# Branch products as three float32r products, and the mixers of a decoder trunk in another order

## The chip, the cores and the metric

The kernel runs on one core of a Trainium2 chip. A core has TensorE (PE, matmuls; PEld is its weight load), VectorE (DVE), ScalarE (ACT), GpSimd (POOL) and SyncE (SP), each with an instruction queue of its own that it works off in order, and 16 DMA engines. The metric is the device time of one execution in microseconds (us).

## What is computed

One layer of a decoder trunk for 512 prompt tokens and 8 x 8 sample tokens (576 together) of width 1024. Four token mixers A to D read one projection, each is projected by a 512 x 1024 matrix, and a sigmoid gate per branch and channel weights the result. Cross attention and a mixture of experts follow; the change does not touch them.

```python
z = jnp.einsum('btd,de->bte', x, p['w_in']) + p['b_in']
u, v, yg, xb, c, q, f, i, go, gz = jnp.split(z, SPLIT_POINTS, axis=-1)
o_a, v_rows = chunk_sgu(u, v, ...)            # A: u * (causal 128x128 mix of LN(v))
xc, conv_new = causal_conv(xb, ...)
h, h_new = rg_lru(xc, h0, ...)                # B: convolution, sigmoids, scan
o_b = jax.nn.gelu(yg) * h
o_c, pool_new = pool_mixer(c, ...)            # C: windows 2, 4, 8, 16
o_d, s_new = hgrn2(q, f, i, go, s0, lb, ...)  # D: gated recurrence, 4 heads
branches = jnp.stack([o_a, o_b, o_c, o_d], axis=2)
proj = jnp.einsum('btgc,gcd->btgd', branches, p['w_branch'])
gates = jax.nn.sigmoid(gz.reshape(B, T, N_BRANCH, D_MODEL))
y = jnp.einsum('btd,de->bte', jnp.sum(gates * proj, axis=2), p['w_out'])
```

## The kernel before

Tokens lie along the free dimension, 576 columns in two halves of 288, channels on the 128 partitions. The mixer phase is a list of steps, `mixer_steps()`, that every engine walks through in the same order; each engine does its own part of a step and waits on semaphores for the others.

- `z` steps project one chunk of 128 channels for one half: 24 matmuls of 128x288 (8 k-tiles, three float32r products each: hi x hi, hi x lo, lo x hi), `split_products`. The weight chunk (1024 x 128, 512 KB) is loaded by SyncE into one of four buffers once the chunk four back is used, and split into a rounded part (`z_weights_hi`) and a rest (`z_weights_lo`) by GpSimd. ScalarE writes the result out with its function (Gelu for `yg`, Silu for `q` and `go`). `kv` steps are float32 products with the memory's weights.
- `hgrn` steps are the four heads of mixer D (called heads 1 to 4 here, numbered 0 to 3 in the code): `prep`, `keys`, `state`, `diag`, `lev0` to `lev8`, `out`, `norm`. At `keys` TensorE transposes an operand that ScalarE and VectorE make; at `lev n` it makes the product of level n-1, from what VectorE wrote at the same step after ScalarE's exponential of the step before. The `z` and `kv` steps fill TensorE between them: `rest` is dealt out over the heads in proportion to the steps' weights.
- Then come `pool` (C), `lru` (B) and `sgu` (A) steps with `merge` units between them, and a loop with the remaining units.
- A `merge` unit (i, u) is half of one chunk of 128 output channels for one branch: a gate product (24 float32r matmuls, bank 0 or 1), a branch product (4 float32 matmuls of 128x288, two records each, bank 2 or 3), ScalarE's sigmoid into `gate`, and VectorE's product, added to `mer`. Branches go D, C, B, A (3 - i). There are 64 units; 32 are written out (`PEEL = 2`), 32 are in the loop. Branch weights have four buffers and are used as they land.
- GpSimd's queue holds the weight splits and, for the pool mixer, the copies into the padded rows `cpad`, which wait for `hg_done`, the output of the four heads.

The diff changes `psum_schedule`, `z_units`, `mixer_steps`, `z_plan` and each engine's `merge_unit`.

## Time and profile before

| | us |
|---|---|
| median of 3 runs | 1592.98 |
| lowest, highest | 1591.44, 1595.31 |
| profiled execution | 1593.02 |
| its span | 1591.2 |
| TensorE busy | 1436.9 (90%) |
| VectorE busy | 782.9 (49%) |
| ScalarE busy | 514.3 (32%) |
| GpSimd busy | 298.1 (19%) |
| weighted products of the branches (512 records) | 134.5 |

The span is the time from the first to the last instruction of the profiled execution; the 1.8 us between it and that execution's own time lie around it. Matmul ends are modelled and matmuls are pipelined, so the distance between two starts tells more than the length of one record. A wait is idle time of an engine, with the instruction that released it.

### The profile page before, as it was taken

The page shows a single profiled execution, that of the slowest core. Times are in us where ns is not written, and L with a number is a line of the kernel's source. Part 1 is how long each engine was busy: PE and PEld are TensorE (multiplying, and loading weights), DVE is VectorE, ACT ScalarE, POOL GpSimd, SP SyncE. Part 2 cuts the span into 40 slices and gives each one's busy share as a digit, 9 for nine tenths or more (in the row PEclk, how much of TensorE's full clock was granted, in tenths as well). Part 3 has the DMA queues.
Part 4 walks back from the last instruction along what each step waited for, and adds up shares of the span by engine and source line. Part 5 has one row for each costly group of instructions (what it writes and reads, how often), then busy time and mean ns, then how long its engine had stood idle before and what let it go on. Part 6 is the DMA issues. An engine that isn't in the chain of part 4 may idle for free.

```text
span 1591.2 us, 20322 instructions
## 1 busy us (share of the span) xinstructions
PE 1436.9 (90%) x8037; PEld 1199.5 (75%) x8037; DVE 782.9 (49%) x1162; ACT 514.3 (32%) x772; POOL 298.1 (19%) x234
## 2 busy tenths in 40 slices
PE   5998889899789788999999989999897799999985
PEld 4887888888778676989998867765685677777762
DVE  6204437362545467632221430244336688887786
ACT  1123341513431343311110011333123566666640
POOL 5111132313314131323332000001000100000030
PEclk9999999998899898999999989999998899999997
DMA  9302232422122121242225311235254699999941
GB/s 328 99 27 74 79 96 77 118 84 78 53 82 71 49 80 40 62 130 80 80 59 195 124 54 53 80 116 207 62 222 153 240 381 394 390 390 396 391 152 61
DMA packets 182172, 234.89 MB, mean 148 GB/s; under 512 B 6224, under 2 KB 125705, under 8 KB 181953
## 3 DMA queue, kind: packets, MB, share of 16 engines
q1 hardware_dynamic: 154848, 170.90, 31.7%
q0 software_dynamic: 12384, 43.56, 8.0%
q10 hardware_dynamic: 14849, 19.16, 3.5%
q8 instruction: 63, 1.03, 0.3%
q14 instruction: 28, 0.23, 0.0%
HBM read 213.98 MB, written 19.36 MB: 147 GB/s over the span
## 4 chain that ended last, share of the span: by engine, by line
PE 48%; DVE 3%; DMA 2%; ACT 2%; issue 1%; POOL 0%; POOLq 0%; DVEq 0%; SPq 0%; ACTq 0%
PE bank L1114 46%; ACT kv_t L744 1%; PE bank L1606 1%; DMA ring<-in_w_out_dram 1%; DMA early_rows<-expert_rows,ints 0%; DVE x_tok L2490 0%; DVE small L1739 0%; DVE x_tok L2496 0%; POOL early_rows L2673 0%; DMA xg<-x_scratch,table 0%; PE bank L1598 0%; PE bank L1138 0%; PE bank L1422 0%; DVE x_tok L2398 0%; DVE x_tok L1751 0%
## 5 line engine op out<-in xcount | busy, mean ns | idle before, releaser
L1114 PE MATMUL bank<-x_hi,z_weights_hi 128*128 128x288 f32 x960 | 307.1, 320 | 9.1 <-DVE ob L1903 5.5
L1114 PE MATMUL bank<-x_lo,z_weights_hi 128*128 128x288 f32 x960 | 290.5, 303 | 0.0
L1114 PE MATMUL bank<-x_hi,z_weights_lo 128*128 128x288 f32 x960 | 290.1, 302 | 0.0
L2232 DVE TENSOR_TENSOR expert_weights_lo<-mring,expert_weights_hi 128x2048 fp32r<-128x2048 f32 x80 | 181.8, 2287 | 54.2 <-ACT expert_weights_hi L1007 54.0
L1114 PEld LDWEIGHTS bank<-x_hi,z_weights_hi 128*128 128x128 f32 x960 | 189.0, 197 | 15.6 <-issue 6.3
L1114 PEld LDWEIGHTS bank<-x_lo,z_weights_hi 128*128 128x128 f32 x960 | 188.6, 196 | 2.6
L1114 PEld LDWEIGHTS bank<-x_hi,z_weights_lo 128*128 128x128 f32 x960 | 187.7, 195 | 0.0
L1007 ACT ACTIVATE expert_weights_hi<-mring 128x2048 fp32r<-128x2048 f32 x80 | 153.4, 1918 | 78.7 <-PE bank L1114 78.7
L2544 POOL CAST z_weights_hi<-z_weights 128x1024 fp32r<-128x1024 f32 x60 | 65.7, 1094 | 592.3 <-PE bank L1114 365.8
L2546 POOL TENSOR_TENSOR z_weights_lo<-z_weights,z_weights_hi 128x1024 fp32r<-128x1024 f32 x60 | 147.4, 2456 | 6.4 <-POOL z_weights_hi L2544 2.9
L1114 PE MATMUL bank<-ob,branch_weights 128*128 128x288 f32 (+1 forms) x512 | 134.5, 405 | 0.0
L906 ACT ACTIVATE gate<-bank,pc 128x288 f32<-128x288 f32 x64 | 31.8, 501 | 255.8 <-PE bank L1114 255.7
L1114 PE MATMUL bank<-expert_weights_hi,xgT_hi 128*128 128x512 f32 x256 | 106.1, 414 | 3.1 <-DVE xgT_lo L2375 3.1
L1114 PEld LDWEIGHTS bank<-ob,branch_weights 128*128 128x128 f32 x512 | 93.3, 189 | 20.3
L1114 PE MATMUL bank<-expert_weights_lo,xgT_hi 128*128 128x512 f32 x256 | 100.5, 393 | 0.0
L1114 PE MATMUL bank<-expert_weights_hi,xgT_lo 128*128 128x512 f32 x256 | 100.3, 392 | 0.0
L2065 DVE TENSOR_TENSOR prod<-gate,bank 128x288 f32<-128x288 f32 x48 | 21.8, 454 | 154.9 <-PE bank L1114 142.5
L1114 PE MATMUL bank<-ring,oT 128*128 128x256 f32 (+1 forms) x320 | 71.2, 381 | 1.1 <-DVE o_rows L2122 1.1
L2656 POOL DMA_INDIRECT xg<-x_scratch,table x16 | 24.8, 1552 | 230.7 <-PE bank L1606 221.0
L1114 PEld LDWEIGHTS bank<-ring,oT 128*128 128x128 f32 (+1 forms) x320 | 56.7, 179 | 13.3 <-issue 2.2
L1114 PE MATMUL bank<-yT,ring 128*128 128x288 f32 x256 | 64.4, 416 | 0.8 <-ACT yT L744 0.8
L1114 PEld LDWEIGHTS bank<-yT,ring 128*128 128x128 f32 x256 | 49.9, 195 | 15.0 <-ACT yT L744 0.9
(419 smaller groups left out, 2303.7 us busy)
## 6 DMA issues: line engine op xcount, KB each, us to landing
mring<-in_e_wg_dram SPq DMA_DIRECT2D x32, 1024.0 KB, 8.5
mring<-in_e_wu_dram SPq DMA_DIRECT2D x32, 1024.0 KB, 9.4
mring<-in_e_wd_dram SPq DMA_DIRECT2D x32, 1024.0 KB, 8.0
z_weights<-in_w_in_dram SPq DMA_DIRECT2D x60, 512.0 KB, 3.9
branch_weights<-in_w_branch_dram SPq DMA_DIRECT2D x32, 256.0 KB, 3.2
kv_k<-in_cache_mem_k_dram POOLq DMA_DIRECT2D x8, 1024.0 KB, 7.6
kv_v<-in_cache_mem_v_dram POOLq DMA_DIRECT2D x8, 1024.0 KB, 5.5
expert_rows<-y_out ACTq DMA_DIRECT2D x14, 512.0 KB, 6.9
```

Of the source, the lines that this page charges most:

```text
L744: act.activation(dst, ps[0:rows, cols[0]:cols[1]] if len(dst.shape) == 2 else ps[0:rows, cols[0]:cols[1]].rearrange("p (a b) -> p a b", a= ...
L906: act.activation(gate[:, b, :], bank[b][:, 0:HALF], ACT.Sigmoid, bias=pc[:, bass.ds(col, 1)]).then_inc(free[b], 1)
L1007: act.activation(m_hi[n % NHI][:], mring[:, chunk_slot[split[n]], :], ACT.Copy).then_inc(m_hi_done, 1)
L1114: return pe.matmul(out, lhsT, rhs, start=start, stop=stop)
L1606: m = pe.transpose(bank[2 + s][:, P * e:P * e + P], xg[:, u, P * c:P * c + P], ident)
L2065: dve.tensor_tensor(prod[:, half, :], gate[:, half, :], bank[nb][:, 0:HALF], ALU.mult).then_inc(free[nb], 1)
L2232: dve.tensor_tensor(m_lo[slot][:], mring[:, slot, :], m_hi[n % NHI][:].bitcast(F32), ALU.subtract).then_inc(m_lo_done, 1)
L2544: pool.tensor_copy(w_hi[hi][:], w_raw[raw][:]).then_inc(g_hi_done, 1)
L2546: pool.tensor_tensor(w_lo[raw][:], w_raw[raw][:], w_hi[hi][:].bitcast(F32), ALU.subtract).then_inc(g_lo_done, 1)
L2656: return pool.indirect_dma_start(xg[:, u, :], None, x2_d, bass.IndirectOffsetOnAxis(ap=index, axis=0))
```

## The change

It does five things.

1. The branch product of a unit becomes 12 float32r matmuls: branch output and branch weights are both split into a rounded part and a rest. ScalarE writes the rounded branch (`branch_hi`, new steps `split`), VectorE the rest (`ob_lo`), per chunk k of four; GpSimd splits each chunk of branch weights behind the gate weights. The branch weights have two buffers instead of four.
2. The spatial mixer (A) moves from last to first: its norms behind `norm` of head 1, its products and outputs into head 3, its splits before and behind `prep` of head 4. Twelve merge units of branch A (chunks 0, 1, 2, 4, 5, 6) stand between the steps of head 4, the other four behind it.
3. The branches are merged in the order A, D, C, B; C is split after each pool output, B after each scan.
4. The loop is gone, all 64 units are written out. The product is written over `gate` and then added to `mer`; only units of the first branch write `mer` at once.
5. `u` is projected before `yg`; the conv, pool and LRU states are written between units.

```diff
+BRANCHES = (0, 3, 2, 1)
+EARLY_D = (0, 1, 2, 4, 5, 6)
+MERGE_D = (EARLY_D + (3, 7),) + (tuple(range(8)),) * 3
...
+    for j in range(KW):
+        rest += [("sgu", "product", j), ("sgu", "out", j)]
+    rest += [("split", 0, j) for j in range(KW)]
+    rest += [("merge", 0, u) for u in range(2 * len(EARLY_D))]
...
+    at = own.index(("hgrn", "norm", 0)) + 1
+    own[at:at] = [("sgu", "norm", j) for j in range(NT + 1)]
...
+    steps += [("split", 1, h) for h in range(KW)]
+    merge(16 - 2 * len(EARLY_D))
...
-        steps.append(("pool", "out", j))
+        steps += [("pool", "out", j), ("split", 2, j)]
...
-        if j:
-            steps.append(("sgu", "norm", 2 * j - 1))
...
+            def branch_hi(i, k):
+                if i == 0:
+                    act.wait_ge(sgu_done, KW)
+                    act.wait_ge(out_stored, 16)
+                elif i == 1:
+                    act.wait_ge(hg_done, KW)
...
+                act.activation(ob_hi[i % 2][:, k, :], ob[:, BRANCHES[i], k, :], ACT.Copy).then_inc(ob_hi_done, 1)
...
+            def branch_lo(i, k):
+                dve.wait_ge(ob_hi_done, splits.index((i, k)) + 1)
+                dve.tensor_tensor(ob_lo[:, BRANCHES[i], k, :], ob[:, BRANCHES[i], k, :], ob_hi[i % 2][:, k, :].bitcast(F32),
+                                  ALU.subtract).then_inc(ob_lo_done, 1)
...
-                    m = mm(bank[2 + half][:, 0:HALF], p_raw[d % 4][:, k, :], rhs, k == 0, k == KW - 1)
+                pe.wait_ge(ob_lo_done, splits.index((i, KW - 1)) + 1)
+                pe.wait_ge(p_lo_done, m + 1)
+                    pairs = ((p_hi[m % 2], hi), (p_hi[m % 2], lo), (p_lo[m % 2], hi))
...
+            def split_gate_weights(m):
+                used(chunk_last(m - 2, "mg") if m >= 2 else z_last[z_split[z_split_last(m)]])
+                split_weights(m % 2, at % ZRING, len(z_split) + m + 1)
+                pool.wait_ge(p_landed[m % 2], 16 * (m // 2 + 1))
+                pool.tensor_copy(p_hi[m % 2][:], p_raw[m % 2][:]).then_inc(p_hi_done, 1)
+                pool.tensor_tensor(p_lo[m % 2][:], p_raw[m % 2][:], p_hi[m % 2][:].bitcast(F32), ALU.subtract).then_inc(p_lo_done, 1)
...
+                elif step[0] == "merge" and step[2] % 2:
+                    split_gate_weights(8 * step[1] + step[2] // 2 + 2)
```

VectorE's queue from the output of head 3 to the keys' operand of head 4 (the row that writes `ob` with `tmp` is the head's output, the last row the keys' operand), before:

```order
L1901 SCALAR_TENSOR_TENSOR tmp<-tmp,pc 128x576
L1903 TENSOR_TENSOR ob<-ob,tmp 128x576
L1797 SCALAR_TENSOR_TENSOR tmp<-f_all,tmp 128x576
L1798 SCALAR_TENSOR_TENSOR tmp<-cst,tmp 128x576
L1801 TENSOR_TENSOR tmp<-tmp 128x512
L1803 TENSOR_TENSOR tmp<-tmp 128x64
L1809 TENSOR_TENSOR f_all<-q_all,tmp 128x576
L1810 COPY small<-tmp 128x4
L1811 COPY small<-tmp 128x8
L1813 TENSOR_TENSOR tmp<-tmp 128x576
```

The same place now, from the head's output on; `conv_odd` rows are the last spatial output.

```order
L1910 TENSOR_TENSOR ob<-ob,tmp 128x576
L2046 TENSOR_TENSOR conv_odd<-bank,sgu_rows 128x512
L2050 TENSOR_TENSOR conv_odd<-bank,sgu_rows 128x64
L2057 TENSOR_TENSOR ob<-ob,conv_odd 128x576
L2079 TENSOR_TENSOR branches_lo<-ob,branch_hi_72 128x576
L1804 SCALAR_TENSOR_TENSOR tmp<-f_all,tmp 128x576
L1805 SCALAR_TENSOR_TENSOR tmp<-cst,tmp 128x576
L2079 TENSOR_TENSOR branches_lo<-ob,branch_hi_72 128x576 x3
L2067 TENSOR_TENSOR mer<-gate,bank 128x288
L1808 TENSOR_TENSOR tmp<-tmp 128x512
L1810 TENSOR_TENSOR tmp<-tmp 128x64
```

A spatial output, four splits and a merge have come between the head's output and the keys; the keys' operand stands four rows further on.

VectorE's queue between two level steps of head 4 (`tmp<-tmp` and `tmp<-q_all,tmp` are the cuts of a level, `mer` is the merge of a unit), before:

```order
L1863 TENSOR_TENSOR tmp<-tmp 128x4x64
L1864 TENSOR_TENSOR tmp<-tmp 128x4x64
L1863 TENSOR_TENSOR tmp<-tmp 128x8x32
L1864 TENSOR_TENSOR tmp<-tmp 128x8x32
L1877 TENSOR_TENSOR tmp<-q_all,tmp 128x4x64
L1878 TENSOR_TENSOR tmp<-tmp 128x4x64
```

And now:

```order
L2067 TENSOR_TENSOR mer<-gate,bank 128x288
L1870 TENSOR_TENSOR tmp<-tmp 128x8x32
L1871 TENSOR_TENSOR tmp<-tmp 128x8x32
L1884 TENSOR_TENSOR tmp<-q_all,tmp 128x4x64
L1885 TENSOR_TENSOR tmp<-tmp 128x4x64
```

The merge of the unit that fills TensorE at `lev0` stands ahead of the cuts of the next level.

GpSimd's queue up to the first two padded rows of the pool mixer, before:

```order
L2544 CAST z_weights_hi_62<-z_weights_54 128x1024
L2546 TENSOR_TENSOR z_weights_lo_58<-z_weights_54,z_weights_hi_62 128x1024
L2562 MEMSET cpad 128x15
L2570 COPY cpad<-ob 128x512
L2571 COPY cpad<-pst 128x8x15
L2572 COPY cpad<-ob 128x8x8
```

And now:

```order
L2601 CAST branch_weights_hi_69<-branch_weights_65 128x512
L2603 TENSOR_TENSOR branch_weights_lo_67<-branch_weights_65,branch_weights_hi_69 128x512
L2555 CAST z_weights_hi_63<-z_weights_55 128x1024
L2557 TENSOR_TENSOR z_weights_lo_59<-z_weights_55,z_weights_hi_63 128x1024
L2601 CAST branch_weights_hi_70<-branch_weights_66 128x512
L2603 TENSOR_TENSOR branch_weights_lo_68<-branch_weights_66,branch_weights_hi_70 128x512
L2578 MEMSET cpad 128x15
L2586 COPY cpad<-ob 128x512
L2587 COPY cpad<-pst 128x8x15
L2588 COPY cpad<-ob 128x8x8
```

Before, the padded rows stand behind the split of one chunk of gate weights, now behind the splits of gate and branch weights of the ninth and the tenth chunk.

## Rows read from the trace of the kernel before

**Rows 1.** Windows: stretch, length, busy (x) of PE, PEld, DVE, ACT, POOL, clock, DMA.
```profile
132.00:404.00 272.00, 244.96 (x1799) 233.92 (x1799) 125.85 (x202) 94.83 (x142) 72.57 (x40) 0.95 0.30 87
404.00:473.50 69.50, 54.03 (x367) 50.28 (x365) 35.80 (x68) 27.63 (x40) 14.13 (x8) 0.92 0.25 70
473.50:538.20 64.70, 55.32 (x305) 48.28 (x305) 31.29 (x74) 10.05 (x15) 24.12 (x27) 0.92 0.22 61
538.20:692.00 153.80, 141.47 (x808) 122.41 (x808) 100.37 (x164) 53.74 (x76) 42.70 (x24) 0.94 0.22 62
692.00:861.30 169.30, 167.90 (x1035) 153.65 (x1036) 40.03 (x68) 18.49 (x36) 51.81 (x33) 0.98 0.30 92
168.30:171.70 3.40, 3.40 (x17) 3.40 (x16) 3.37 (x2) 0.35 (x1) 3.32 (x2) 0.50 0.31 93
```

**Rows 2.** TensorE's waits, 130 to 960 us: total, times, longest.
```profile
PE bank L1114 <- DVE tmp L1878: 20.9, 11, 3.3
PE bank L1232 <- DVE tmp L1813: 18.5, 4, 5.5
PE bank L1114 <- DVE tmp L1981: 12.0, 2, 6.5
PE bank L1114 <- DVE ob L1903: 5.5, 1, 5.5
PE bank L1114 <- DVE conv_odd L1981: 4.0, 1, 4.0
...
PE bank L1114 <- issue: 2.8, 2, 1.9
...
PE bank L1371 <- DVE tmp L2038: 2.2, 2, 1.6
...
PE bank L1114 <- ACT gate L906: 1.4, 1, 1.4
```

**Rows 3.** Timeline of TensorE in the closing loop: start, us, instruction.
```profile
762.45 2.10 PE L1114 MATMUL bank<-ob,branch_weights 128*128 x8
764.17 0.51 PE L1114 MATMUL bank<-x_hi,z_weights_hi 128*128 128x288 f32 x1
764.52 0.29 PE L1114 MATMUL bank<-x_lo,z_weights_hi 128*128 128x288 f32 x1
```

**Rows 4.** Timeline of GpSimd: one weight chunk split in two.
```profile
476.81 1.12 POOL L2544 CAST z_weights_hi<-z_weights 128x1024 fp32r<-128x1024 f32 x1
478.01 2.39 POOL L2546 TENSOR_TENSOR z_weights_lo<-z_weights,z_weights_hi 128x1024 fp32r<-128x1024 f32 x1
```

**Rows 5.** Part 6 of the page: DMA issues, KB each, us to landing.
```profile
branch_weights<-in_w_branch_dram SPq DMA_DIRECT2D x32, 256.0 KB, 3.2
```

**Rows 6.** Timeline of VectorE: one output of the spatial mixer, first and last row.
```profile
683.78 0.68 DVE L2038 TENSOR_TENSOR tmp<-bank,sgu_rows 128x512 f32<-128x512 f32 x1
...
684.69 0.76 DVE L2049 TENSOR_TENSOR ob<-ob,tmp 128x576 f32<-128x576 f32 x1
```

**Rows 7.** Tile x_hi, ScalarE: count, shortest, median, longest in ns.
```profile
L811 ACT ACTIVATE x_hi<-xT x8: 667/668/684, 49.6 to 53.6; 128x576 fp32r<-128x576 f32 x8
```

**Rows 8.** Timeline of ScalarE in prep of head 4.
```profile
399.76 1.28 ACT L837 ACT_TABLE_LOAD   x1
401.06 0.78 ACT L837 ACTIVATE tmp<-tmp,small 128x576 f32<-128x576 f32 x1
```

**Rows 9.** Timeline of VectorE at a level of head 4.
```profile
436.43 0.42 DVE L1878 TENSOR_TENSOR tmp<-tmp 128x256 f32<-128x256 f32 x1
436.76 0.68 DVE L1887 TENSOR_TENSOR att_m<-bank,cst 128x512 f32<-128x512 f32 x1
```

**Rows 10.** Timeline of VectorE: first and last row of the fourth pool window.
```profile
513.21 0.90 DVE L1923 TENSOR_TENSOR csum<-cpad 128x710 f32<-128x710 f32 x1
...
518.28 0.22 DVE L1941 COPY att<-cpad 128x120 f32<-128x120 f32 x1
```

**Rows 11.** Timeline of VectorE: start of the third LRU convolution.
```profile
593.27 2.57 DVE L1977 TENSOR_SCALAR tmp<-xpad,pc 128x512 f32<-128x512 f32 x1
```

More of the change, by code:

```diff
@@ L133, in psum_schedule @@
             (low if step[0] in ("z", "kv") else high)(name)
-    for b in range(4):
-        count[b] += (4 - PEEL) * 8
     turn["low"] = 0
@@ L214, in mixer_steps @@
             steps.append(rest.pop(0))
-    units = [("merge", i, u) for i in range(PEEL) for u in range(16)]
+    at = [steps.index(step) for step in (("hgrn", "state", KW - 2), ("sgu", "out", 0), ("sgu", "out", KW - 1),
+                                         ("hgrn", "keys", KW - 1))]
+    assert at == sorted(at) and steps.index(("merge", 0, 0)) > steps.index(("hgrn", "norm", KW - 2))
+    units = [("merge", 0, u) for u in range(2 * len(EARLY_D), 16)] + [("merge", i, u) for i in range(1, 4) for u in range(16)]
+    late = []
     def merge(count):
         for _ in range(count):
-            if units:
-                steps.append(units.pop(0))
+            steps.append(units.pop(0))
+            if steps[-1] == ("merge", 1, 15):
+                steps.extend(late)
+                late.clear()
+    steps += [("split", 1, h) for h in range(KW)]
+    merge(16 - 2 * len(EARLY_D))
     for j in range(KW):
@@ L242, in mixer_steps @@
         steps.append(("lru", "scan", j))
-        if j < KW - 1:
-            steps.append(("sgu", "norm", 2 * j))
+        (late if units[0][1] == 1 else steps).append(("split", 3, j))
         if j < KW - 1:
@@ L247, in mixer_steps @@
         merge(1)
-    merge(1)
-    for j in range(KW):
-        steps.append(("sgu", "product", j))
-        merge(1)
-        steps.append(("sgu", "out", j))
+    steps.append(("states",))
     merge(len(units))
-    steps.append(("states",))
     return steps
@@ L290, in step_units @@
         return ["oc", "op", "oq"]
-    if step[1] != "product":
+    if step[0] in ("merge", "split") or step[1] != "product":
         return []
@@ L303, in z_plan, with branch_splits @@
                     names.append(name)
-                last[name] = step_units(step)[0]
+                last[name] = f"mg{step[1]}_{step[2]}" if step[0] == "merge" else step_units(step)[0]
     return names, last
+def branch_splits():
+    return [step[1:] for step in mixer_steps() if step[0] == "split"]
 def weight_plan():
```

244 lines of the change are left out of this document (113 added, 131 removed).

## Prediction

> **What bounds the kernel now.** First the stretches of the span, then TensorE's waits by cause, then single timelines. TensorE is busy for nearly all of each mixer stretch [rows 1]: the four heads of the gated recurrence run from 132 to 473.5 us, pool, LRU and spatial mixers with 32 units from 473.5 to 692, the closing loop with the other 32 to 861.3. So time is TensorE work, plus its waits, plus what the halved clock costs. From 130 to 960 us it waits 20.9 us in 11 places for the level products' operands (tmp L1878), 18.5 in 4 for the keys (L1813), 12.0 and 4.0 for the LRU convolution, 5.5 for the last head's output, 2.8 before pool products (issue), 2.2 and 0.6 for the last spatial rows, 1.4 for a gate [rows 2]. The granted clock, read as its missing share times each stretch, costs 0.05 x 272 + 0.08 x 69.5 + 0.08 x 64.7 + 0.06 x 153.8 + 0.02 x 169.3 = 37 us [rows 1]. Outside 132 to 861 nothing changes.
>
> **The products.** A unit is a gate product of 24 float32r matmuls and a branch product of 4 float32 ones, 8 records. In the loop the 8 start at 762.45 and the next unit at 764.17: 1.72 us. The first float32r start after them takes 0.35 us to the next, where such starts are else 0.13 apart [rows 3]: 0.22 more. Twelve float32r matmuls at 0.1325 are 1.59, so a unit falls by 1.72 + 0.22 - 1.59 = 0.35, and 64 of them by 22.4. Twelve units now stand alone between small float32 products and pay such a change of type again: about 2 back. Term: **-20.5** (bounds -16, if the pace is 0.14, and -24).
> The trace shows 8 records in 1.72 us for 4 products, 0.43 each, 3.25 float32r steps. The Trainium skill, FP8 and Floating Point Precision, TensorE Precision Notes, says that true FP32 makes four passes. By that a product were 4 x 0.1325 = 0.53 us, the 64 units would save 256 x 0.1325 = 34, and the sum would be some 13 lower. The trace does not agree.
> GpSimd also splits the branch weights. Its cast of 128x1024 takes 1.12 and its subtraction 2.39 [rows 4], so half the size is 0.56 + 1.2; a chunk costs 3.5 + 1.8 + about 0.3 = 5.6 us against two units, 2 x 4.8 = 9.6. The branch weights have two buffers and load when the product two chunks back is done, 3.2 us to landing [rows 5]: split some 6 us after that product, wanted 12.8 after it. Hidden, about 7 to spare.
>
> **The keys, and the start of head 4.** The keys' operand comes only after ScalarE has emptied the fill ahead of it, so heads 2 and 3 keep waits of 4.3 and 5.5. Ahead of head 4 it is another thing. Fills are dealt by count, and count now includes steps without matmul work; after `norm` of head 3 TensorE has only a spatial product (1.35) and the first gate product (3.2). The branch product needs all four splits of the spatial branch, which stand around `prep` on ScalarE and VectorE. From the end of the norm product: head output 5.0 (5.5 in [rows 2], less 0.4 of a table load that can now run ahead); last spatial output on VectorE 1.67 (683.78 to 685.45), to 6.6 [rows 6]; ScalarE copy of 128x576 0.67 [rows 7]; `prep` on ScalarE with three table loads of 1.28, and four activations of 0.6 to 0.8 [rows 8], to 13.9; VectorE's two operations 2.1; three subtractions 0.76 each, to 18.4. TensorE is free at 4.6: it waits 13.9. The product, at half clock, ends at 21.4, and behind it VectorE's gate product, keys and ScalarE's exponential reach 25.0: 3.6 more. Keys: 4.3 + 5.5 + 13.9 + 3.6 + the unchanged 4.3 = 31.6, against 18.5: **+13.1** (bounds +6 and +18).
> The row has table loads at 1.28 us. The Trainium skill, ScalarE: Activation LUTs, What ACT_TABLE_LOAD costs, gives about 2.7; by it the chain's three loads would put 4 us more here. The measured row decides.
>
> **The levels.** Head 1 and 2 get denser fills and wait where a slot is empty: 3.7 (such a wait with a table load in it was 3.3 from the modelled end [rows 2]) + 1.7 and 1.8 + 1.2 = 8.4. In head 3 the fill is used up at the third level; from there VectorE's chain sets the pace, one level being four cuts of 0.42 and a mask and sum of 0.68 each, 3.1 us [rows 9], 3.8 at the small levels, against 0.8 to 1.35 of TensorE work, with three spatial outputs of 1.67 in VectorE's queue. Step by step: 0.1 + 3.0 + 1.1 + 4.0 + 1.3 + 3.5, and 0.9 + 0.6 at output and norm = 14.5. In head 4 every fill is now a unit whose product VectorE must merge before it comes to the next level: after the branch product 0.45 until it starts, 0.45 merge, four cuts 1.4 = 2.4 us in which TensorE has nothing. Five such, 0.9 and 1.5 where no fill stands, 0.7 at the state: 15.1. Sum 38.0 against 20.9: **+17.1** (bounds +8, if VectorE ran ahead at half of them, and +24).
> At the end of head 4 four units cover the 5.5: **-5.5**.
>
> **Pool.** GpSimd now writes the padded rows behind the split of the tenth chunk, whose branch weights load only after the eighth chunk's last product: 3.5 to land, 1.8 + 0.3 split, 1.2 pads, 2.5 window = 9.5 from there, TensorE filled for 4.8: wait 5.2 with the drain. For the next three VectorE's queue between a unit and the next pool product is merge 0.95 (two operations, one before), output 1.0, then new: ScalarE's copy 0.67 with hand-overs 0.2, subtraction 0.76, then the window, 3.5, 4.4, 5.3 (the last is 513.21 to 518.50 [rows 10], the others one and two sums of 0.9 shorter, as is the first above with 2.5). Less the filling unit of 4.8 that gives 3.6, 4.1, 4.7. Together 17.6 against 2.8: **+14.8** (bounds +6 and +19).
>
> **LRU and states.** The spatial norms no longer stand ahead of the second and third convolution, 3.5 us each, and no gate waits for them; the subtraction that replaces them is 0.76, and a fill is 0.3 shorter. First product 7.2, then 0.8, 1.2, 1.2 = 10.4 against 12.0 + 4.0 + 1.4: **-7.0**. The states go between units: 0.5 for 2.8, **-2.3**.
>
> **Sum:** -20.5 + 13.1 + 17.1 - 5.5 + 14.8 - 7.0 - 2.3 - 7 + 5 + 2 = +9.7. The profiled execution's 1593.0 becomes 1602.7, said as 1603; its 1593.02 (span 1591.2) is within 0.1 of the median of the three, 1592.98, so nothing is scaled.
>
> **The rivals.**
> *The waits close.* A fill in head 4 is longer now (4.8 for 3.2) and may hide the level chain. For it: VectorE is only half busy there, 35.8 of 69.5 us, and TensorE idles 15 [rows 1], which the new fills could take. It decides if VectorE reaches a level's cuts before the fill ends; the order of its queue, merge first, speaks against. Then +17.1 falls to about 0 and half of the keys' term and its clock go: 1603 - 17 - 7 - 3 = 1576; with half of that, 1589. **Faster**, 0.17.
> *Four passes.* If each float32 product were worth four float32r steps, the term of the products would be 34 and the time 1603 - 13.4 = 1589.6, on the edge of faster and same; rows 3 show 3.25 steps, 3.7 with the change of type. That is the rule of FP8 and Floating Point Precision in the Trainium skill. 0.04, half to each side.
> *It evens out.* One of the two terms, pool or levels, lies at its lower bound (9 less each) and the other between: 1603 - 9 = 1594, down to 1590. Same, 0.15.
> *GpSimd sets the pace.* If loading and splitting took over 9.6 us a chunk, 32 chunks would each be late. From rows 4 and 5 it is 5.6 and 3.2 in parallel with spare; at 10.5 it would be 32 x 0.9 = 29 more, 1631. 0.04.
> *The forecast,* waits outweigh products, 0.60.
>
> **How the numbers follow.** Slower by over 0.2% (3.2 us, about what a measurement of this kernel can tell) is 0.60 + 0.04 = 0.64; same 0.15 + 0.02 = 0.17; faster 0.17 + 0.02 = 0.19. The range leaves out the fully closed waits and the GpSimd case, and takes waits closed by somewhat over half (-18) and the upper bounds of levels, pool and clock together (+7 + 4 + 9, of which I take 17): 1585 to 1620.
>
> **What would show it.** Right: branch products of 12 records 0.13 apart; a TensorE wait of over 10 us in the first branch product; waits near 2.4 us after each unit in head 4; 4 to 5 us before each pool product; the two LRU waits of 5.5 and 4.0 nearly gone; a closing run of 20 units at 4.8. Wrong: head 4 without waits above 2, pool products without wait, a closing pace above 5.

## The result and the profile after

The changed kernel takes 1634.6 us (median of four runs, 1632.1 to 1640.0) against 1594.1 for the kernel before beside it: ratio 1.0258, interval 1.0227 to 1.029. The profiled execution took 1634.13, its span 1632.3. Forecast were 1603 and a range of 1585 to 1620: slower was right, the size was not. Between the two profiled executions the loss is 41 us and not 10.

The stretches of the changed kernel, in the windows' columns of [rows 1]. Its mixer phase ends some 41 us later, so the same clock times hold earlier work; the granted clock is what to read first.

```profile
136.00:404.00 268.00, 247.93 (x1853) 239.30 (x1852) 107.70 (x184) 86.90 (x134) 80.94 (x46) 0.96 0.32 90
404.00:473.50 69.50, 40.47 (x253) 36.83 (x251) 40.16 (x70) 29.95 (x39) 11.98 (x8) 0.77 0.15 41
473.50:538.20 64.70, 51.80 (x299) 47.70 (x300) 27.33 (x48) 20.29 (x25) 16.07 (x12) 0.79 0.16 46
538.20:692.00 153.80, 117.17 (x731) 107.68 (x730) 68.22 (x126) 32.48 (x49) 57.39 (x50) 0.84 0.16 47
692.00:861.30 169.30, 158.02 (x1131) 151.78 (x1131) 102.22 (x142) 53.83 (x80) 84.04 (x60) 0.97 0.30 87
```

Until 404 little differs. From 404 to 692 TensorE is busy 209 of 288 us and granted 0.77 to 0.84, where [rows 1] have 251 of 288 and 0.92 to 0.94: the loss is waits there, and with them clock. (Half clock, below, is a granted clock of 0.50, 1.2 GHz for 2.4.) GpSimd is busy 157 us from 473.5 to 861 for 119.

TensorE's waits from 100 to 1000 us, in total, times, longest, to be laid beside [rows 2] (the line numbers are those of the changed kernel: L1885 are the level operands, L1820 the keys, L1988 the convolutions, "issue" is here the waits before the four pool products, 21.2 together, and one of 0.5 elsewhere):

```profile
PE bank L1129 <- DVE tmp L1885: 36.9, 16, 7.3
PE bank L1129 <- issue: 21.6, 5, 6.1
PE bank L1247 <- DVE tmp L1820: 17.4, 4, 5.7
PE bank L1129 <- DVE branches_lo L2079: 13.3, 1, 13.3
PE bank L1129 <- DVE tmp L1988: 11.6, 2, 7.8
PE bank L1129 <- DVE conv_odd L1988: 6.8, 2, 4.1
```

The levels grew by 16, the pool products from 2.8 to 21.2, the first branch product waits 13.3, and the convolutions, forecast at 10.4 in all, wait 18.4.

Three starts of a gate product in the closing run, one unit each:

```profile
830.71 0.30 PE L1129 MATMUL bank<-x_hi,z_weights_hi 128*128 128x288 f32 x1
835.49 0.29 PE L1129 MATMUL bank<-x_hi,z_weights_hi 128*128 128x288 f32 x1
840.23 0.30 PE L1129 MATMUL bank<-x_hi,z_weights_hi 128*128 128x288 f32 x1
```

They are 4.78 and 4.74 apart. Before, the same distance is this:

```profile
799.98 0.51 PE L1114 MATMUL bank<-x_hi,z_weights_hi 128*128 128x288 f32 x1
805.08 0.51 PE L1114 MATMUL bank<-x_hi,z_weights_hi 128*128 128x288 f32 x1
```

5.10. A unit gained 0.34, as forecast (0.35), and the first matmul no longer takes 0.51: the change of type is gone.

Head 4's start and the pool products on TensorE (the wait and its releaser in brackets):

```profile
473.45 0.61 PE L1129 MATMUL bank<-branch_hi,branch_weights_hi 128*128 128x288 f32 x1 [13.31 <-DVE branches_lo L2079]
473.86 0.44 PE L1129 MATMUL bank<-branches_lo,branch_weights_hi 128*128 128x288 f32 x1
...
479.72 0.69 PE L1247 MATMUL bank<-cst,tmp 128*128 128x128 f32 x2 [3.02 <-DVE tmp L1820]
```

```profile
611.39 2.37 PE L1129 MATMUL bank<-ob,wp 128*128 128x512 f32 x4 [4.33 <-issue]
...
647.85 2.37 PE L1129 MATMUL bank<-ob,wp 128*128 128x512 f32 x4 [5.84 <-issue]
667.52 2.36 PE L1129 MATMUL bank<-ob,wp 128*128 128x512 f32 x4 [6.12 <-issue]
```

The branch product that ends the 13.3 us wait runs at half clock (0.24 between starts), and so does each of the four pool products after its wait (the second, left out here, waits 4.86): 2.4 us, where the same product took 1.26 before.

### The profile page after: what moved, and what is told of

Read it like the earlier page. It is cut to its first block, busy times and chain, and to the rows that moved or that the text cites. A ratio compares the mean times of both kernels' runs of the same rounds, so it can differ in the third digit from the quotient of the medians.

```text
span 1632.3 us, 20440 instructions
## 1 busy us (share of the span) xinstructions
PE 1431.0 (88%) x8293; PEld 1216.2 (75%) x8293; DVE 807.8 (49%) x1178; ACT 538.1 (33%) x799; POOL 364.4 (22%) x298
## 4 chain that ended last, share of the span: by engine, by line
PE 53%; DVE 8%; issue 4%; ACT 4%; DMA 2%; POOL 0%; POOLq 0%; DVEq 0%; SPq 0%; ACTq 0%
PE bank L1129 50%; ACT kv_t L742 1%; PE bank L1613 1%; DMA ring<-in_w_out_dram 1%; DVE mer L2074 1%; DMA early_rows<-expert_rows,ints 0%; DVE tmp L2002 0%; DVE x_tok L2500 0%; DVE small L1746 0%; DVE x_tok L2506 0%; ACT L906 0%; DMA xg<-x_scratch,table 0%; DVE gate L2072 0%; POOL early_rows L2689 0%; PE bank L1605 0%
## 5 line engine op out<-in xcount | busy, mean ns | idle before, releaser
L1129 PE MATMUL bank<-x_hi,z_weights_hi 128*128 128x288 f32 x960 | 298.6, 311 | 1.9 <-POOL z_weights_lo L2557 1.3
L906 ACT ACTIVATE gate<-bank,pc 128x288 f32<-128x288 f32 x64 | 31.5, 500 | 239.9 <-PE bank L1129 229.8
L1129 PE MATMUL bank<-branch_hi,branch_weights_hi 128*128 128x288 f32 x256 | 76.1, 297 | 13.4 <-DVE branches_lo L2079 13.3
L2072 DVE TENSOR_TENSOR gate<-gate,bank 128x288 f32<-128x288 f32 x48 | 21.7, 452 | 124.5 <-PE bank L1129 88.9
L1129 PE MATMUL bank<-tmp 128*128 128x128 f32 (+1 forms) x248 | 41.9, 320 | 39.4 <-DVE tmp L1885 36.9
L1129 PE MATMUL bank<-branches_lo,branch_weights_hi 128*128 128x288 f32 x256 | 76.1, 297 | 0.0
L1129 PE MATMUL bank<-branch_hi,branch_weights_lo 128*128 128x288 f32 x256 | 75.9, 296 | 0.0
L1129 PEld LDWEIGHTS bank<-tmp 128*128 128x128 f32 (+1 forms) x248 | 36.0, 221 | 44.8 <-DVE tmp L1885 40.2
```

Of the source, the lines that this page charges most:

```text
L906: act.activation(gate[:, b, :], ps[:, 0:HALF], ACT.Sigmoid, bias=pc[:, col:col + 1]).then_inc(fr, 1)
L1129: return pe.matmul(out, lhsT, rhs, start=start, stop=stop)
L2072: dve.tensor_tensor(gate[:, half, :], gate[:, half, :], ps[:, 0:HALF], ALU.mult).then_inc(fr, 1)
```

## Experiments

### The order, the products and the splits taken apart

Three kernels stand between the kernel before and the changed one. The first has the new order with the old products.

```diff
-                pe.wait_ge(ob_lo_done, splits.index((i, KW - 1)) + 1)
-                pe.wait_ge(p_lo_done, m + 1)
+                pe.wait_ge(p_landed[m % 2], 16 * (m // 2 + 1))
...
-                    pairs = ((p_hi[m % 2], hi), (p_hi[m % 2], lo), (p_lo[m % 2], hi))
+                    ins = mm(ps[:, 0:HALF], p_raw[m % 2][:, k, :], ob[:, BRANCHES[i], k, cols], k == 0, k == KW - 1)
...
-                act.activation(ob_hi[i % 2][:, k, :], ob[:, BRANCHES[i], k, :], ACT.Copy).then_inc(ob_hi_done, 1)
...
-                pool.tensor_copy(p_hi[m % 2][:], p_raw[m % 2][:]).then_inc(p_hi_done, 1)
```

> The changed kernel's order with the branch products of before: four float32 matmuls from the branch output and the landed weights, no split of branch or branch weights on ScalarE, VectorE or GpSimd. Theory (the products save about 20 us, the splits cost nearly as much in waits): products +20.5; the wait of 13.3 in the first branch product falls to about 2, but the keys of head 4 then wait some 7 longer, -5; pool waits 1.65 shorter each, -6; LRU waits back near 0 to 1, -7; clock -3: about 1634, the same as the changed kernel. Rival (the splits are hidden and the order alone makes the waits): all of the 20 us come on top, 1650 to 1655. Other rival (the products gained less than 20, for the clock was halved beside many of them): below 1620.

Measured 1607.0 (ratio to before 1.0087, 1.0064 to 1.0111). The theory (1634) and the first rival (1650) were wrong. The time lies in the band of the second rival, below 1620, and the next run bears out that the products gain less than 20, but not through the clock, as it had it. The changed kernel is 27.7 slower than its own order with the old products: the splits cost more than the products give back. What is left to the order alone is 13.5.

The second adds TensorE's side of the change alone (the edit against the run before it).

```diff
-                    ins = mm(ps[:, 0:HALF], p_raw[m % 2][:, k, :], ob[:, BRANCHES[i], k, cols], k == 0, k == KW - 1)
+                    for n in range(3):
+                        ins = mm(ps[:, 0:HALF], x_hi[:, k, 0:P], (x_hi, x_lo)[n % 2][:, k, cols], k == 0 and n == 0,
+                                 k == KW - 1 and n == 2)
```

> The run with float32 products, with twelve float32r matmuls of 128x288 in the place of each four float32 ones, but from operands that are there anyway (the input's rounded part and rest), so no split of branch or weights is made and the branch products are left out of the result. It has TensorE's gain from the change without its price. Theory (0.35 us a unit, forecast -20.5 with bounds -16 and -24): 1607 - 20 = 1587, unit distance in the closing run 4.75 for 5.1. Rival (shorter fills only make the waits longer: in head 4 and between pool and LRU steps 40 units fill the waits, and only the closing units give their gain in full): 1607 - 10 = 1597.

Measured 1593.9 (ratio 0.9995, 0.9978 to 1.0011): 13.1 below the run before it, between theory and rival. In the closing run a unit takes 4.77 for 5.11, so TensorE's work fell by some 20, but in the stretches where another engine sets the pace a shorter unit only uncovers more of the wait. Half clock is not the reason: from 100 to 1000 us it holds for 102 us in the run before and 99 in this one. The waits of the two, first with float32 products, then with the stand-in:

```profile
PE bank L1121 <- DVE tmp L1880: 32.4, 16, 4.0
PE bank L1239 <- DVE tmp L1815: 21.9, 4, 7.5
PE bank L1121 <- DVE tmp L1983: 9.1, 2, 6.7
PE bank L1121 <- issue: 8.0, 5, 3.2
...
PE bank L1121 <- DVE conv_odd L1983: 1.6, 2, 1.0
```

```profile
PE bank L1121 <- DVE tmp L1882: 33.3, 15, 4.0
PE bank L1239 <- DVE tmp L1817: 22.4, 4, 7.9
PE bank L1121 <- issue: 10.8, 5, 3.9
PE bank L1121 <- DVE tmp L1985: 9.9, 2, 7.1
PE bank L1121 <- DVE conv_odd L1985: 3.1, 2, 1.7
```

The lines are 0.5 to 2.8 longer, together 6.5, which is about what the 20 lack.

The third has the splits of the branches (ScalarE, VectorE) as in the changed kernel, but not GpSimd's splits of the branch weights.

```diff
-                    pairs = ((p_hi[m % 2], hi), (p_hi[m % 2], lo), (p_lo[m % 2], hi))
+                    pairs = ((x_hi, hi), (x_hi, lo), (x_hi, hi))
...
-                pool.tensor_copy(p_hi[m % 2][:], p_raw[m % 2][:]).then_inc(p_hi_done, 1)
...
-                pool.tensor_tensor(p_lo[m % 2][:], p_raw[m % 2][:], p_hi[m % 2][:].bitcast(F32), ALU.subtract).then_inc(p_lo_done, 1)
```

> The changed kernel without GpSimd's cast and subtraction of the branch weights; the branch products take the input's rounded part as weights, so their result is not the branch products. TensorE's work and the splits of the branches on ScalarE and VectorE are as in the changed kernel. It stands between the stand-in run (1593.9, no split at all) and the changed kernel (1634.6). Theory (GpSimd's share is stretched VectorE rows, which cost 11.6 us for the subtraction alone, the branch splits' share is the hole before the first branch product and the queue before the pool products): GpSimd 15 to 18 of the 40.7, so 1617 to 1620; the fifth level wait of head 3 (7.3) back at 4.0, the last three LRU waits under 3 each. Rival (the subtraction was all of it and the cast costs nothing): 1623. Other rival (GpSimd is nearly all): below 1610.

Measured 1608.2 (ratio 1.0109, 1.0076 to 1.0141). So the 40.7 between the stand-in and the changed kernel divide into 14.3 for the branch splits and 26.4 for GpSimd. (The run's interval leaves some 5 us of play in this division.) The theory had 15 to 18 for GpSimd and the first rival 1623; the time lies in the band of the second rival, below 1610. GpSimd's two operations, 1.9 us a chunk and never themselves waited for in the closing run, are the dearer part. The longest level wait is back at 4.0, and the convolutions wait 13.9 for 18.4:

```profile
PE bank L1127 <- DVE tmp L1883: 33.4, 15, 4.0
...
PE bank L1127 <- issue: 15.5, 5, 5.5
PE bank L1127 <- DVE tmp L1986: 10.5, 2, 7.7
PE bank L1127 <- DVE branches_lo L2077: 10.2, 1, 10.2
PE bank L1127 <- DVE conv_odd L1986: 3.4, 2, 2.0
```

(The wait for `branches_lo` is 13.3 in the changed kernel and 10.2 here, but the gate product ahead of it ran at full clock there and at half clock here. VectorE is ready at the same point after the head's output in both; half clock inside a stretch that waits anyway cost nothing here.)

### GpSimd beside VectorE

VectorE and then GpSimd in the changed kernel, where the second and the third convolution are made late (start, us, instruction):

```profile
706.22 0.46 DVE L2072 TENSOR_TENSOR gate<-gate,bank 128x288 f32<-128x288 f32 x1
706.71 1.96 DVE L2074 TENSOR_TENSOR mer<-mer,gate 128x288 f32<-128x288 f32 x1
...
710.30 1.29 DVE L1988 SCALAR_TENSOR_TENSOR conv_odd<-xpad,pc,conv_odd 128x64 f32<-128x64 f32 x1
...
739.98 2.36 DVE L1988 SCALAR_TENSOR_TENSOR tmp<-xpad,pc,tmp 128x64 f32<-128x64 f32 x1
```

```profile
705.85 2.50 POOL L2557 TENSOR_TENSOR z_weights_lo<-z_weights,z_weights_hi 128x1024 fp32r<-128x1024 f32 x1
...
709.91 1.60 POOL L2603 TENSOR_TENSOR branch_weights_lo<-branch_weights,branch_weights_hi 128x512 fp32r<-128x512 f32 x1
...
739.59 2.67 POOL L2557 TENSOR_TENSOR z_weights_lo<-z_weights,z_weights_hi 128x1024 fp32r<-128x1024 f32 x1
```

The add into `mer`, 0.46 elsewhere, starts at 706.71 and ends at 708.67; GpSimd's subtraction ends at 708.35. The 128x64 row, 0.28 elsewhere, starts at 710.30 and ends at 711.59; GpSimd's ends at 711.51. At 739.98 it is 2.36, to 742.34; GpSimd ends at 742.26. A VectorE operation with two operands in SBUF that starts inside one of these GpSimd operations ends just behind it, while the product from a bank at 706.22 is not touched. That holds for the whole stretch from 130 to 1000 us: of 68 such rows that start inside a cast or a subtraction of weights with over 0.3 us of it left, 67 are at least 0.15 us longer than the shortest of their form and end 0.1 to 1.1 us behind GpSimd; of 46 rows that read a bank in the same place none is longer. The longest level wait, 7.33, ends behind such rows too: a cut of 0.46 starts at 430.60 and takes 2.48, inside a subtraction that ends at 432.76. The Trainium skill, SBUF — State Buffer, section SBUF: two separate sides, calls the pair of ports that VectorE and GpSimd share an exclusive lock for the whole instruction, for VectorE operations with two SBUF inputs among others. These rows agree, to 0.3, 0.1 and 0.1 us.

Shortening one of GpSimd's operations (1.3 us to 0.25) tests it with all other work in place:

```diff
-                pool.tensor_tensor(p_lo[m % 2][:], p_raw[m % 2][:], p_hi[m % 2][:].bitcast(F32), ALU.subtract).then_inc(p_lo_done, 1)
+                pool.tensor_tensor(p_lo[m % 2][:, :, 0:8], p_raw[m % 2][:, :, 0:8], p_hi[m % 2][:, :, 0:8].bitcast(F32), ALU.subtract).then_inc(p_lo_done, 1)
...
-                    pairs = ((p_hi[m % 2], hi), (p_hi[m % 2], lo), (p_lo[m % 2], hi))
+                    pairs = ((p_hi[m % 2], hi), (p_hi[m % 2], lo), (p_hi[m % 2], hi))
```

> The changed kernel with GpSimd's subtraction for the branch weights cut to 8 of 128 columns (about 0.2 us for 1.2), and the third branch product made with the rounded weights, so the weights' rest is left out of the result; TensorE's work is the same. Theory (GpSimd's extra 1.2 us per chunk stretches VectorE's operations, and that is where the LRU waits of 2.7, 3.8 and 4.1 us come from that were forecast at 0.8, 1.2 and 1.2): these three fall to under 2 each, the pool waits a little, time 8 to 12 us lower, about 1624. Rival (the waits are VectorE's own queue, with one more row per merge and the split): no more than 3 us lower, waits as they are.

Measured 1623.0 (ratio 1.0197, 1.0176 to 1.0218), 11.6 lower, as the theory has it. The longest level wait fell from 7.3 to 4.3, the pool products' from 21.6 to 18.0, the convolutions' from 18.4 to 15.4; the three that were to fall below 2 are 1.8, 2.8 and 3.1, so only partly. 1.0 of the pool's 3.6 is the first pool wait, which is shorter because GpSimd comes to the padded rows sooner and not because VectorE runs freely. The other 14.8, down to the run with unsplit weights, belong to the cast and what is left of the subtraction. Little of them is waits (2.5 before the pool products, 1.5 at the convolutions), while half clock goes from 137 to 109 us; with the four executions of this run between 1618.7 and 1627.3 the split between the two operations is rough.

```profile
PE bank L1129 <- DVE tmp L1885: 33.3, 15, 4.3
PE bank L1129 <- issue: 18.0, 5, 5.5
...
PE bank L1129 <- DVE tmp L1988: 10.5, 2, 7.7
...
PE bank L1129 <- DVE conv_odd L1988: 4.9, 2, 3.1
```

### What the clock costs

Unused matmuls, whose result nobody reads, are put ahead of the waits, each into the bank that the product behind the wait overwrites. In both kernels:

```diff
+            def warm(name):
+                ps, _ = acquire(pe, name)
+                for _ in range(WARM[name]):
+                    mm(ps[:, 0:HALF], x_hi[:, 0, 0:P], x_hi[:, 0, 0:HALF], True, True)
...
+                        warm(f"L{h}{n}")
                         pe.wait_ge(hg_x, len(LEVELS) * h + n + 1)
```

> The changed kernel with unused float32r matmuls (128x288, 0.13 us each at full clock) put ahead of 28 of TensorE's waits between 130 and 780 us, as many as nine tenths of each wait hold, into the bank that the next product overwrites. Nothing else changes. Theory (the halved clock after the waits is the mis-sized term: it is granted for 143 us between 130 and 780 in the changed kernel and 78 before, and costs half of the busy share of it): granted clock near 1.00 in all stretches to 980, time 30 to 45 us lower, 1590 to 1604. Rival (the clock cost about what was forecast, 5 more than before, or follows something else than idle time): under 10 us lower and the low stretches stay; if the unused matmuls delay the next products instead, slower.

> The kernel before with the same unused float32r matmuls ahead of 21 of its waits between 130 and 640 us. Theory: its 78 us at half clock go, 25 to 33 us lower, 1561 to 1569; then the changed kernel with its waits filled is slower than this one by what waits less products make without the clock, about 24 us. Rival (the clock costs little): within 10 us of 1594.

Measured 1600.4 for the changed kernel (ratio 1.0045, 1.0028 to 1.0061), 34.2 lower as the theory has it, and 1578.1 for the kernel before (0.9896, 0.9873 to 0.9919), 15.4 lower where 25 to 33 were expected. Stretches of each, in the windows' columns, first three of the changed one:

```profile
132.00:404.00 272.00, 268.48 (x2069) 259.20 (x2068) 114.67 (x197) 92.73 (x142) 81.93 (x46) 1.00 0.32 92
404.00:582.00 178.00, 168.73 (x1213) 160.78 (x1214) 86.99 (x149) 66.66 (x88) 53.68 (x38) 0.97 0.17 48
582.00:780.00 198.00, 192.12 (x1378) 184.16 (x1377) 128.71 (x207) 60.72 (x88) 89.95 (x73) 0.99 0.21 61
```

The last two of the kernel before, filled:

```profile
404.00:582.00 178.00, 172.37 (x1115) 155.45 (x1114) 93.72 (x183) 56.19 (x82) 49.31 (x43) 0.99 0.23 65
582.00:780.00 198.00, 190.95 (x1194) 172.55 (x1194) 95.91 (x158) 43.09 (x68) 59.22 (x34) 1.00 0.29 83
```

The same stretches without the added matmuls, changed kernel, are granted 0.96, 0.80 and 0.89:

```profile
132.00:404.00 272.00, 248.40 (x1853) 239.78 (x1854) 109.90 (x188) 89.19 (x137) 81.80 (x46) 0.96 0.32 90
404.00:582.00 178.00, 128.69 (x783) 119.12 (x782) 82.77 (x147) 61.96 (x79) 40.50 (x30) 0.80 0.15 42
582.00:780.00 198.00, 158.11 (x1020) 144.97 (x1019) 119.44 (x191) 53.66 (x79) 84.02 (x69) 0.89 0.20 56
```

Summed from the clock's records between 100 and 1000 us, half clock holds for 154 us in the changed kernel and 27 with its waits filled, 89 and 24 in the kernel before. A us at half clock costs 34.2 / 126 = 0.27 there and 15.4 / 65 = 0.24 here. These prices are net: what the unused matmuls themselves held up, if anything, is in them. Of the 41 us between the kernels 18.8 are clock by these two runs: with waits filled they are 22.3 apart.

### The queue in head 4

VectorE makes the product of an early unit after its part of the head's next step:

```diff
+            held = []
             for step in steps:
+                if step[0] == "merge" and step[1] == 0 and step[2] < 2 * len(EARLY_D):
+                    held.append(step)
+                    continue
                 if step[0] == "hgrn":
                     hgrn(step[1], step[2])
+                    while held:
+                        merge_unit(*held.pop(0)[1:])
```

> The changed kernel, where VectorE makes the products of the twelve units in head 4 behind its part of the head's next step and no longer ahead of it. Theory (the waits of 2.5, 3.4, 2.1, 3.9, 2.2, 1.3 in head 4 are there because VectorE merges a unit, 0.45, and only then comes to four cuts, 1.4, after the branch product): VectorE's cuts then run while TensorE does the unit, the six waits of 15.4 fall to under 4, and with the clock that they cost (0.3 us per us at half clock) 13 to 18 us are saved: about 1619. Rival (the chain through ScalarE's exponentials and VectorE's cuts is itself as long as a unit, the order is no matter): under 4 us, 1631 to 1635.

Measured 1607.2 (ratio 1.0073, 1.0045 to 1.01), 27.4 lower, where 13 to 18 were expected. The six level waits of head 4, 15.4 together, are 1.1, 0.8 and nothing. The keys of head 4 no longer wait 3.0 either, nor the state 1.7, which the expectation had left out, since the first merge no longer stands ahead of the keys' operand: three waits for the keys are left. These waits, 19 us together, and 24 us less at half clock (130 for 154) make up most of the 27.4.

```profile
PE bank L1129 <- DVE tmp L1885: 22.6, 11, 6.4
...
PE bank L1247 <- DVE tmp L1820: 14.4, 3, 5.7
```

So the forecast's mechanism for the levels of head 4 was right and could be taken away: the waits came from the order in one queue, not from the chain's length.

### The pool mixer

```diff
-        steps += [("pool", "out", j), ("split", 2, j)]
...
         steps.append(("pool", "window", j))
+        if j:
+            steps.append(("split", 2, j - 1))
...
-                if step == ("pool", "window", 0):
+                if step == ("merge", 0, 13):
                     pool.wait_ge(hg_done, KW)
```

> The changed kernel, where each split of the pool branch stands behind the next pool window and not ahead of it, and GpSimd writes the first two padded rows ahead of the splits of the ninth and tenth weight chunk. Theory (forecast's terms: copy, hand-overs and subtraction, 1.65 each, and the late pads, 5.2): waits before the pool products fall from 4.3, 4.9, 5.8, 6.1 to about 0, 3.2, 4.1, 4.5, so 9 us, with the clock 10 to 12, about 1623. Rival (VectorE is late because its sums are stretched beside GpSimd's splits, the place of the splits is no matter): the last three stay above 4.5 and the time within 5 us of 1634.

Measured 1623.3 (ratio 1.0176, 1.0149 to 1.0203), 11.4 lower, as the theory has it. The waits before the four pool products went from 4.33, 4.86, 5.84, 6.12 to 1.11, 3.48, 4.32, 5.13; the first is the late pads, the others 1.4, 1.5 and 1.0 each for 1.65. The first product now runs at full clock (1.26) and two others only partly at half (1.85, 1.54 for 2.37), hence 11.4 for 7.1 us of waits.

### Head 1's keys

The keys of head 1 start at 135.5 in the changed kernel and at 132.2 before. One of GpSimd's loads, the spatial bias rows, now stands at the head of its queue; here it is moved back.

```diff
-            load_rows(sgu_rows[:], sgu_b[0].rearrange("g t -> (g t)"), ld_sgu)
...
                     load_rows(sg_g[:], sgu_g[0], ld_sgu)
+                    load_rows(sgu_rows[:], sgu_b[0].rearrange("g t -> (g t)"), ld_sgu)
```

> The changed kernel with the load of the spatial bias rows moved from the head of GpSimd's queue to where the other two rows of the spatial mixer are loaded. Theory (the keys of head 1 start at 135.5 for 132.2 because this load stands ahead of the parameters on GpSimd's queue): they start near 132 again, 3 us less, 1631. Rival (the shift is in the first 104 us of any run and not tied to this load): no change of the keys' start or the time.

Measured 1635.6 (two executions): no gain, though the keys start at 132.9. The run with merges later has the load in its old place and the start at 136.8, the one with the short rest at 133.9. The start varies from run to run by as much as the effect, so the load explains nothing that the times show.

### Everything mended, and a mix of both kernels

The changed kernel with the later merges, the pool order and the filled waits:

> The changed kernel with three mends at once: VectorE's merges behind the next step in head 4, the pool order (split behind the next window, pads first), and unused matmuls ahead of the waits that are left. Theory (levels, pool and clock are separate terms): 1634.6 less 27, 11 and some 27 for the clock = 1570, below the kernel before (1594) but above it less its own clock cost only if the first hole, the keys and the LRU waits still cost more than the products save: within 10 of 1578. Rival (the terms are the same time counted twice, a mend in head 4 only moves the waits behind it): above 1585.

Measured 1575.3 (ratio 0.9885, 0.9858 to 0.9912). That is 59.3 lower than the changed kernel; the two mends alone gave 27.4 and 11.4, which leaves 20.5 for the filled waits, less than their 34.2 since there were fewer waits left. It beats the kernel before, and stands level with that one once its own waits are filled (1578.1).

Then float32r products only where no mixer waits behind them, in the 16 units of the last branch, together with the later merges of head 4 (the padded rows stay where they were, though the expectation names them):

```diff
+                if i < 3:
...
+                    pe.wait_ge(p_landed[m % 2], 16 * (m // 2 + 1))
+                    for k in range(KW):
+                        ins = mm(ps[:, 0:HALF], p_raw[m % 2][:, k, :], ob[:, BRANCHES[i], k, cols], k == 0, k == KW - 1)
...
+                    return
...
+                if m < 24:
+                    return
                 pool.wait_ge(p_landed[m % 2], 16 * (m // 2 + 1))
...
-        (late if units[0][1] == 1 else steps).append(("split", 3, j))
+    steps += [("split", 3, j) for j in range(KW)]
```

> The changed order with float32 products for the first three branches and float32r products for the last branch alone, whose 16 units follow the LRU mixer without a wait between them; branch splits only there (ScalarE and VectorE before the states, GpSimd for the last eight chunks); VectorE's merges in head 4 behind the next step, pads first. Theory (float32r products pay where no wait follows and their splits have cover): 1607 - 24 (merges later) - 5.6 (16 x 0.35) - 1 = 1577. Rival (the gain of the later merges was bound to the longer units of the changed kernel): 1590 or more.

Measured 1573.5 (ratio 0.9861, 0.9844 to 0.9879), near the theory's 1577. No run has this order and the later merges with float32 products throughout, so what the 16 units give by themselves (5.6 were expected) is not shown. With its waits filled by a table that fits those of the run with float32 products (27 matmuls for its 4.0 of the fifth level, 46 for the 6.7 of the first convolution) and not its own:

> The run before this one with unused matmuls ahead of its remaining waits. Theory (about 85 us at half clock between 130 and 700, 0.3 us each): 22 to 27 lower than it, 1550 to 1557, faster than the kernel before with its waits filled (1578). Rival (the clock gain does not add to shorter waits): within 12 of the run before.

Measured 1575.8 (ratio 0.9879, 0.9861 to 0.9897), a miss: not faster at all. The four splits had gone from the list that the fills are dealt from, so the fills, TensorE's work between the steps, fell to other steps, and the unused matmuls stood where nothing waited while part of the real waits stayed: half clock fell from 92 to 34 us and the time did not. With the table read from the mix's own trace (a number is that of the unused matmuls ahead of one wait: `kdT` the keys, `L22` level 2 of head 3, `mg0_0` the last spatial product, `pp` the pool, `rp` the LRU):

```diff
-WARM = {'kdT0': 30, 'kdT1': 40, 'kdT2': 30, 'kdT3': 48, 'L00': 23, 'L04': 12, 'L11': 8, 'L12': 10, 'L15': 6, 'L21': 18,
-        'L23': 20, 'L24': 27, 'L26': 18, 'L31': 6, 'pp1': 9, 'pp2': 15, 'pp3': 21, 'rp0': 46, 'rp1': 4, 'rp2': 16, 'rp3': 6}
+WARM = {'kdT0': 30, 'kdT1': 30, 'kdT2': 36, 'kdT3': 16, 'L02': 17, 'L06': 16, 'L11': 12, 'L15': 21, 'L22': 17, 'L26': 28,
+        'L33': 8, 'mg0_0': 36, 'pp1': 9, 'pp2': 15, 'pp3': 21, 'rp0': 45, 'rp1': 4, 'rp2': 16, 'rp3': 5}
```

> The mixed version (float32r products for the last branch only, merges later) again with unused matmuls, now ahead of the 18 waits that its own trace shows, since in the version with the first table they stood partly where another dealing of the steps leaves no wait. Theory (an unused matmul pays in a wait of its length and costs its 0.13 us elsewhere): about 80 us at half clock go at 0.3 each and nothing is added, 1573.5 - 20 = 1553. Rival (the clock gain is used up: the time of shorter fills comes back as longer waits): 1565 or more.

Measured 1560.6 (ratio 0.9789, 0.977 to 0.9808), the fastest of all, 12.9 under the mix without them for 51 us less at half clock (0.25 a us), some 8 short of the theory. Half clock is 41 us here, more than in the miss, so it is the places that differ. One long wait stays:

```profile
PE bank L1128 <- DVE conv_odd L2074: 5.1, 1, 5.1
```

## Why the forecast was right in sign and wrong in size

By its own terms, forecast and then measured (waits from the two traces):

| term | forecast | measured |
|---|---|---|
| products | -20.5 | 64 x 0.34 = -21.8 |
| keys, start of head 4 | +13.1 | 30.7 for 18.5, +12.2 |
| levels | +17.1 | 41.5 for 20.9, +20.6 |
| end of head 4 | -5.5 | -5.5 |
| pool | +14.8 | 21.2 for 2.8, +18.4 |
| LRU | -7.0 | 18.4 for 17.4, +1.0 |
| states | -2.3 | 0.3 for 2.8, -2.5 |
| basis | -7 | 0 |
| clock | +5 | +18.8 |
| port | +2 | inside the rows above |
| sum | +9.7 | +41.2 |

**Right.** The products: the twelve records are 0.13 apart, the unit fell to 4.76. The trace's own row (0.43 per float32 product) decided rightly against the case of 0.53 per product, which would have shown a gain of 0.5 a unit. The start of head 4 came as it was worked out from the end of the norm product, 13.3 for 13.9 and 3.0 for 3.6, and so did heads 1 and 2 (8.7 for 8.4) and the six waits of head 4 (with the state 17.1 for 15.1). Moving the merge in VectorE's queue removed these six but for 1.9 us, and the 3.0 and 1.7 too, which shows their cause; the 13.3 has no such run.

**By how much.** The forecast is 31.5 short. By the table 13.8 of them are the clock, 8.0 the LRU, 7 the basis, 3.6 the pool, 3.5 the levels; the other terms take 4.4 back. GpSimd's price, 26.4, is another cut through the same us and not to be added to these: some 14 of it are longer waits in the rows of levels, pool and LRU, and some 12 are clock, since half clock falls from 154 to 109 us without GpSimd's weight splits (44 x 0.27).

**Wrong: the clock, +5 for +18.8.** The term counted waits above 2.4 us: a dozen before, 14 after and five at the edge. The trace before has 12 of 2.44 and more, the one after 21, and seven were not among the 14: three after units in head 4 (2.5, 3.4, 3.9), three of the LRU (2.7, 3.8, 4.1) and one more in head 3 (2.6). Half clock held for 65 us more. It also holds longer at a time, 13.7 us from 428 in head 3 and 20.5 from 462, over the long wait and the start of head 4, where small steps stand between waits. Beside it the price was read wrongly. The forecast took the missing share of the clock times the stretch, 37 us for the kernel before, 3 a wait. Filling its waits removed 65 of its 89 us at half clock and gave 15.4. Half clock costs about a quarter of its length and not half. Part of it lies in waits (11 of the 20.5 us from 462), and what TensorE does faster the next wait can take back; that this is the whole reason is argued and not run. At that price, +5 stands for 20 us more at half clock.

**Wrong: the port, 2 for most of 26.** The forecast looked at one stretched row [rows 11] and at GpSimd's total (58 us more, of which "a part of it beside chains on the path"). The run without GpSimd's weight splits puts their price at 26.4, that with the short subtraction 11.6 of it. The waits that it lengthens are that of the fifth level in head 3, 7.3 for a forecast 4.0 (4.0 without the splits), three of the pool's, 3.2 of the 4.4 by which they are longer than forecast, and the LRU's, 18.4 for 13.9 without them. The first pool wait, 4.3 for 1.4, belongs to the 26.4 too but not to the port: GpSimd comes to the padded rows later, which the forecast had (5.2). The step that failed is named by this: durations were taken from rows where VectorE stood alone, and only one term was added for all the places where it does not.

**Wrong: the LRU, beside the port.** Its four waits are 10.7 together in the run with float32 products, 13.0 with the stand-in, 13.9 with the branch splits, 18.4 with GpSimd's; forecast were 10.4. So beside the 4.5 of GpSimd's splits 2.3 come with the shorter units and 0.9 with the branch splits, of which the forecast had taken in too little (0.3 less a fill, one subtraction).

**Wrong: the pool's working.** The listed pieces do not give the stated waits: 0.95 + 1.0 + 0.87 + 0.76 and a window of 3.5, 4.4 or 5.3, less the unit of 4.8, are 2.3, 3.2 and 4.1 and not 3.6, 4.1 and 4.7. That the stated ones came near the run without GpSimd's splits (3.6, 4.6, 5.5) is luck as far as its working goes. Put in as the pieces have it, the forecast would have been 2.9 us lower.

**Wrong: the basis, 7.** It was taken off because measured waits run from the modelled end of a matmul, and the table finds no such gap. The single waits came out at or above the forecast ones where that difference should have put them 0.3 to 0.6 below; only at the start of head 4 did it show (0.6 twice).

**The rivals.** "The waits close" and "it evens out" did not happen, but the first was nearly to be had: with the merges behind the steps the waits in the levels of head 4 close. "GpSimd sets the pace" was wrong in its mechanism. No product of the closing run waited for a chunk, and GpSimd's queue had time to spare there; yet its figure, 1631, was nearest, by luck, since GpSimd cost mainly by blocking VectorE and, but for the first pool wait, not by its own pace.

**And where the gain went.** From before to changed: order +13.5, TensorE's faster products -13.1 (of 20, the rest turned into waits), branch splits +14.3, GpSimd's splits +26.4.

## What to carry to other kernels

A cheaper matmul pays in full only where TensorE never waits; price the operand splits on the other engines first, and put them where cover is long (the mix did so in the last branch, though no run shows that branch's gain by itself). When GpSimd gets new work, go through VectorE's chains on the path and ask at each whether a two-operand row can start inside a GpSimd operation; count each such hit with what is left of GpSimd's operation. Count waits by what follows them too: about a quarter of a us at half clock is lost here, and unused matmuls ahead of the waits, as many as the wait holds and read from that very kernel's trace, gave 1.0% in the kernel before and 2.1% in the changed one.

## What the hardware showed beyond that

A GpSimd cast, one operand read and one written, holds VectorE up as the subtraction does: in the changed kernel 18 of 19 VectorE rows with two operands in SBUF that start inside a cast of weights with over 0.3 us left are stretched, and 49 of 49 inside a subtraction. Cast and subtraction were not timed apart: a run with the subtraction shortened saves 11.6 of the 26.4 us, none has the subtraction without the cast. And half clock that fell into a stretch which waits for another engine was free: the gate product ahead of the 13.3 us wait ran at full clock there and at half clock in the run with unsplit weights (a wait of 10.2), with the same end.
